# One-core transformer kernel: norm epsilon from a memset, first weight block in two transfers, and its copy moved between the two row tiles

## The reference, cut to what matters

```python
def _rmsnorm(x, g):
    x32 = x.astype(F32)
    y = x32 * lax.rsqrt(jnp.mean(x32 * x32, axis=-1, keepdims=True) + NORM_EPS)
    return (y * g.astype(F32)).astype(x.dtype)
...
def _moba(x, w_qkv, w_o):
    ...
    qkv = jnp.einsum('bsd,de->bse', x, w_qkv).reshape(b, s, 3, h, dh)
```

## Time and profile before

| | us |
|---|---|
| median of 3 runs | 826.84 (826.57 to 828.23) |
| profiled execution, its own time | 830.34 |
| its span in the trace | 828.6 |
| PE busy in the span | 769.8 |
| DVE busy | 486.1 |
| ACT busy | 375.4 |

### The profile page before, as it was taken

How to read it: one execution, slowest core, us unless ns; L and a number is a source line. 1 busy time by engine, 2 the same in 40 slices (tenths; PEclk the granted TensorE clock), 3 DMA queues, 4 the chain that set the end, 5 groups by cost and what they waited for, 6 DMA issues and landing times.

```text
span 828.6 us, 16218 instructions
## 1 busy us (share of the span) xinstructions
PE 769.8 (93%) x6678; PEld 646.5 (78%) x6678; DVE 486.1 (59%) x842; ACT 375.4 (45%) x572; POOL 55.0 (7%) x94
## 2 busy tenths in 40 slices
PE   7999999999999999999999999999999787686876
PEld 6999998999999998999998999899855443343432
DVE  4555667767766778857764344487875423324245
ACT  4555764554554556467553554464432212111123
POOL 2300041000000000200111000000010000000000
PEclk9999999999999999999999999999999988888789
DMA  9964362555555654534343132459989999999992
GB/s 301 293 206 138 117 191 77 202 179 175 202 168 187 203 170 136 198 108 153 121 136 100 56 103 102 153 163 403 420 330 421 420 421 419 421 420 420 420 418 84
DMA packets 89027, 193.82 MB, mean 234 GB/s; under 512 B 3630, under 2 KB 69521, under 8 KB 76546
## 3 DMA queue, kind: packets, MB, share of 16 engines
q1 hardware_dynamic: 86640, 186.66, 60.8%
q0 software_dynamic: 1888, 4.61, 1.8%
q10 hardware_dynamic: 434, 1.62, 0.5%
HBM read 191.83 MB, written 1.05 MB: 233 GB/s over the span
## 4 chain that ended last, share of the span: by engine, by line
PE 72%; DMA 18%; DVE 5%; ACT 2%; issue 1%; SPq 1%; DVEq 0%; ACTq 0%
DMA expert_w<-in_expert_w_up 17%; PE PG L2045 15%; PE PG L2047 14%; PE PG L2046 14%; PE PG L2654 3%; PE PM L2045 3%; PE PM L2047 3%; PE PM L2046 3%; PE PM L2684 2%; PE PM L2505 1%; ACT whi L853 1%; PE PG L2676 1%; SPq L679 1%; DMA raw<-in_moba_w_qkv 1%; PE PM L2130 1%
## 5 line engine op out<-in xcount | busy, mean ns | idle before, releaser
L2045 PE MATMUL PG<-hT_hi,whi 128*128 128x256 f32 (+1 forms) x816 | 235.5, 289 | 1.5 <-DVE hT_lo L1382 1.4
L2047 PE MATMUL PG<-hT_hi,wlo 128*128 128x256 f32 (+1 forms) x816 | 230.4, 282 | 0.0
L2046 PE MATMUL PG<-hT_lo,whi 128*128 128x256 f32 (+1 forms) x816 | 230.3, 282 | 0.0
L1364 DVE TENSOR_TENSOR wlo<-raw,whi 128x2048 fp32r<-128x2048 f32 x73 | 167.2, 2290 | 66.7 <-ACT whi L853 66.5
L2045 PEld LDWEIGHTS PG<-hT_hi,whi 128*128 128x128 f32 x816 | 153.8, 189 | 7.9 <-issue 4.6
L2047 PEld LDWEIGHTS PG<-hT_hi,wlo 128*128 128x128 f32 x816 | 154.1, 189 | 0.0
L2046 PEld LDWEIGHTS PG<-hT_lo,whi 128*128 128x128 f32 x816 | 153.6, 188 | 0.2
L853 ACT ACTIVATE whi<-raw 128x2048 fp32r<-128x2048 f32 x73 | 139.4, 1910 | 22.3 <-PE PG L2047 19.9
L2654 PE MATMUL PG<-expert_w,xw 128*32 128x256 f32 x992 | 75.4, 455 | 38.5 <-DMA expert_w<-in_expert_w_up 38.5
L2654 PEld LDWEIGHTS PG<-expert_w,xw 128*32 128x32 f32 x992 | 37.0, 126 | 61.6 <-issue 50.4
L1956 DVE SCALAR_TENSOR_TENSOR y_lo<-PG,small,y_hi 128x512 fp32r<-128x512 f32 x16 | 12.0, 750 | 97.5 <-ACT y_hi L1283 97.5
(11 more groups left out here) (529 smaller groups left out, 1339.2 us busy)
## 6 DMA issues: line engine op xcount, KB each, us to landing
expert_w<-in_expert_w_gate SPq DMA_DIRECT2D x32, 1024.0 KB, 26.6
expert_w<-in_expert_w_up SPq DMA_DIRECT2D x32, 1024.0 KB, 26.8
expert_w<-in_expert_w_down SPq DMA_DIRECT2D x32, 1024.0 KB, 26.8
raw<-in_ffn_w_up SPq DMA_DIRECT2D x22, 1024.0 KB, 5.0
raw<-in_w_in SPq DMA_DIRECT2D x22, 1024.0 KB, 5.0
raw<-in_moba_w_qkv SPq DMA_DIRECT2D x12, 1024.0 KB, 5.8
raw<-in_ffn_w_down SPq DMA_DIRECT2D x11, 1024.0 KB, 4.8
raw<-in_moba_w_o SPq DMA_DIRECT2D x4, 1024.0 KB, 5.1
```

The costliest lines, as they stand in the source:

```text
L1364: dve.tensor_tensor(lo_of(n), raw[:, n % R, :], hi_of(n).bitcast(F32), ALU.subtract).then_inc(s_lo, 1)
L2045: pe.matmul(dst, lh, rh, start=start, stop=False, **kw)
L2046: pe.matmul(dst, lh, rl, start=False, stop=False, **kw)
L2047: return pe.matmul(dst, ll, rh, start=False, stop=stop, **kw)
```

## The change

Three edits. The epsilon of the first norm is a column of `vrow` that POOL fills by a second memset, so ACT's square root waits for `s_row_mix` 18 (two memsets and the row `norm_mix`) in place of the constants. Granule 0 comes in two transfers of 128 x 4 x 256; the first half raises `s_first_hi`, the second `landed[0]`. ACT and DVE take the first half of granule 0 between the turned rows of tile 0 and those of tile 1. PE's order is the same.

```diff
-        ones_row = vrow[0:1, 0, :]
+        ones_row, eps_first = vrow[0:1, 0, :], vrow[:, 1, 0:1]
...
-            for i in range(12):
+            for i, done in enumerate((s_first_hi, landed[0])):
+                k = slice(KH * i, KH * i + KH)
+                sp.dma_start(raw[:, 0, GR // 2 * i:GR // 2 * i + GR // 2].rearrange("p (k n) -> p k n", k=KH), wqkv[:, k, 0:256]).then_inc(done, 16)
+            for i in range(1, 12):
...
             pool.memset(ones_row, 1.0).then_inc(s_row_mix, 1)
+            pool.memset(eps_first, RMS_EPS).then_inc(s_row_mix, 1)
...
-                    act.activation(rt[:, i:i + 1], ss[:, i:i + 1], ACT.Sqrt, scale=1.0 / D, bias=con("eps6")).then_inc(s_rt, 1)
+                    act.activation(rt[:, i:i + 1], ss[:, i:i + 1], ACT.Sqrt, scale=1.0 / D, bias=con("eps6") if q else eps_first).then_inc(s_rt, 1)
...
             norm_sq(0)
-            act.wait_ge(s_cst, 16)
+            act.wait_ge(s_row_mix, 18)
             norm_sqrt(0, [0])
             norm_sq(1)
             norm_sqrt(0, [1])
-            act.wait_ge(landed[0], 16)
+            norm_hi(0, [0])
+            act.wait_ge(s_first_hi, 16)
             act.activation(hi_of(0)[:, 0:GR // 2], raw[:, 0, 0:GR // 2], ACT.Copy).then_inc(s_first_hi, 1)
-            norm_hi(0)
+            norm_hi(0, [1])
+            act.wait_ge(s_cst, 16)
...
-                        dve.wait_ge(s_row_mix, 18)
+                        dve.wait_ge(s_row_mix, 19)
...
             norm_apply(0)
+            norm_lo(0, [0])
             c = slice(0, GR // 2)
-            dve.wait_ge(s_first_hi, 1)
+            dve.wait_ge(s_first_hi, 17)
             dve.tensor_tensor(lo_of(0)[:, c], raw[:, 0, c], hi_of(0)[:, c].bitcast(F32), ALU.subtract).then_inc(s_first_lo, 1)
-            norm_lo(0)
+            norm_lo(0, [1])
...
-            pe.wait_ge(s_row_mix, 17)
+            pe.wait_ge(s_row_mix, 18)
```

## The result

The change is **slower**: median 829.8 us (828.09 to 832.57, 11 runs) against 827.57 us (826.57 to 828.5, 11 runs of the kernel before beside it). The ratio is 1.0024, 95% interval 1.0014 to 1.0033, some 2 us. The forecast was no change, 827.2, with a range up to 828.6. The profiled execution took 832.57 us with a span of 830.8.

A forecast was written before the change was run, and what follows sets the result against it. PE was taken to bound the kernel (72% of the chain), its start held by granule 0's landing. Epsilon 0, transfers 0, order +0.36 and 0 behind it gave 827.2 us, called no change, range 825.8 to 828.6.

The forecast's parts named there:

- step 3 of the part on the order: On DVE: first half's lo waits for ACT's copy at 12.32, then runs 12.35 to 13.58.
- +0.36: New order on ACT and DVE: PE's first real multiplication starts at 14.32 against 13.96, 0.36 us later.
- The clock rival: PE's hole grows from 1.40 to 1.76, TensorE drops to 1.2 GHz: costs 2.15, 829.35 us; chance 0.07.
- The signs set beforehand: Changed profile: transposes at 8.78, first-half copy 11.3, PE 14.3; wrong if transposes move or copy starts before 11.
- The epsilon gains nothing: ACT's square root starts 1.09 earlier, but PE is in `keep_warm` until 8.78: gain on the path 0.
- Nothing between granule 0 and the experts absorbed the shift: No transfer stands on the chain there, so a shift of PE's start moves all that follows equally, once.
- The price of a second transfer: One more issue on SP ahead of granules 1 and 2: taken as 0, bounds 0 and 0.6 us.
- The late-landing rival: Granule 0 lands later in most runs, which only the kernel before pays fully: 825.8 to 827.2 us; chance 0.22.

The follow-up runs named there:

- Run 3: The change, with GpSimd's subtraction made to wait until DVE has done its own; ratio 1.0015 to the kernel before.
- before's second profile: The kernel before, unchanged, run and profiled again; PE starts at 13.51, first expert load at 558.24, ratio 0.9996.
- run 10: The kernel before, with PE also waiting for granule 1's lo and `keep_warm(24)` in place of `keep_warm(3)` filling the hole; ratio 1.0040.
- run 9: The kernel before, with PE also waiting for granule 1's lo before it starts granule 0, hole unfilled; ratio 1.0066 to the kernel before.
- the order alone: The kernel before with only the new order on ACT and DVE, epsilon and transfers as before; ratio 1.0019.
- run 4: The change with fourteen instead of three idle multiplications behind the transposes, filling PE's hole; ratio 1.0019 to the kernel before.
- run 7: The kernel before with only the epsilon taken from the memset; ratio 0.9997.
- run 8: The kernel before with only granule 0 split into two transfers; ratio 0.9997.

## Why the prediction was wrong

**What failed is step 3 of the part on the order**: "The lo of the first half waits for 12.32, runs 12.35 to 13.58". The wait was right, the 1.23 us was not. It came from a row of before in which DVE's subtraction began at 10.79 and POOL's at 10.86. DVE was first by 0.07, so its duration was undisturbed and POOL's 3.39 held a wait of 1.02 (3.39 less the 2.37 that it takes when it is first). In the new order POOL is first, and the wait falls to DVE, which is on the path. The rows that show the overlap were there to read, and POOL's 3.39 for a subtraction as large as DVE's of 1.23 was taken as its own speed. Run 3 shows it: POOL moved away, 1.23 is back.

**The size.** Counted from the constants, the forecast had PE's start at 7.41 (14.32 less 6.91). The change's profiles show 8.21, 7.95 and 8.23, later by 0.54 to 0.82, and DVE's subtraction is longer by 0.58 to 0.86: nothing else was mis-sized in the order. Against before's second profile (13.51) the start moved by 1.02 to 1.35, where +0.36 was forecast. At one to one (run 10) this is 0.12 to 0.16%. The measured interval, 0.14 to 0.33%, begins there. Of the 2.6 us between 827.2 and 829.8, 0.7 doesn't come from the change at all: the forecast stood on a median of three runs of the kernel before, 826.84, and eleven gave 827.57.

**The clock rival had 0.07 and came true in two of three profiles.** Its price was near: 2.15 forecast, 2.1 in run 9, and in the change's own profiles 2.9 (first load 4.13 behind before's second profile, 1.26 of it the start) and 1.6 (2.92 less 1.35). Its chance was set for a hole of 1.76; the conflict made it 1.9 to 2.6 in the change and 2.9 with the order alone. The Trainium skill, page "TensorE: Matmul & The Clock Gate", section "Part 1: The HAM clock gate", says that the windows over which the chip judges run freely and don't start with the kernel, so that the point of a change of level varies with where in a window the work falls. The runs agree in that like holes, 2.64 and 2.58, gave both outcomes.

How often does it fall in the runs behind the median? No trace shows them, but the record has each run's mean granted clock. In the change's two sets of 11 runs, the ten longest (829.80 to 832.57) have 0.967 or 0.968 and the twelve shortest (827.96 to 829.18) 0.969 to 0.971. The medians of these two groups are 830.46 and 828.34, 2.1 us apart, which is the price of run 9. With the hole filled, 1 run of 11 is under 0.969. This speaks for a fall in somewhat less than half of the change's runs, and for a loss made up of the later start and, in those runs, the clock. It is no proof: the mean takes in the whole span, before's first profile has 0.968 with the full level at 15 to 20, and 14 of 94 runs of the kernel before are under 0.969 too. And how much of the median is the clock's stays **open**, since run 4, whose runs hardly show a fall, is no faster than the change within 0.1%.

**The signs set beforehand.** Two of them came true by the letter: the transposes moved (8.43, not 8.78) and ACT's copy started before 11 (10.87). Neither was the fault. Counted from the constants the copy came at 4.31 where the forecast has 4.35 (11.26 less 6.91); the signs were set as absolute times, and the start of this profile was 0.35 earlier. The sign that did tell, multiplications at the spacing of the lower level, was the clock's. No sign was set on the length of DVE's subtraction.

**What held.** The epsilon gains nothing while `keep_warm` stands in front of the transposes (run 7). The transposes moved only with the constants: 8.43, 1.87 behind 6.56, as 8.78 behind 6.91. Nothing between granule 0 and the experts absorbed the shift. The price of a second transfer was taken as 0 and is no loss (run 8). The late-landing rival failed: landings do move by 0.44, but the granule and the constants moved together (2.79 apart in the first profile of before, 2.85 in the second), so neither order gains on the other in them.

## What to carry to other kernels

When an instruction is moved, look at what runs beside it at its new place, and don't take its duration from a row where it had started first: in these runs two subtractions with all operands in SBUF, one on DVE and one on GpSimd, ran one after the other. A duration that is long for its size, such as 3.39 us beside 1.23, may be a wait inside the busy time. And at the start of a kernel count from a common event, here the constants: they landed between 6.26 and 6.91 in the fourteen profiles, and the start of the change's PE, less what DVE's subtraction took over 1.23, was 7.37 behind them in all three profiles.

## What the runs showed of the hardware

DVE's subtraction with both inputs in SBUF and GpSimd's copy or subtraction, which read SBUF too, exclude each other for a whole instruction. The one that starts first runs at its own speed (DVE's 1.22 to 1.23, GpSimd's copy 1.04 and its subtraction 2.35 to 2.38). In seven profiles DVE's half-granule subtraction, started while GpSimd worked, ended 1.07 to 1.09 us after GpSimd's instruction (for example 12.95 and 14.02, 12.65 and 13.74, 10.14 and 11.21), and GpSimd's, started behind DVE's, ended 2.21 to 2.24 after it (before: 12.02 and 14.25). DVE's `hT_lo` pieces, with one operand in PSUM, kept their 0.68 to 0.69 beside GpSimd's work, though their other operand, `hT_hi`, is in SBUF. The wait shows inside the length of the blocked instruction and not as idle time in front of it. The Trainium skill, page "SBUF — State Buffer", section "SBUF: two separate sides", has this rule: a DVE operation with two SBUF inputs and a GpSimd operation that reads SBUF compete for an exclusive lock held for the whole instruction. The runs agree in every case. By that rule, with the durations of these runs on the forecast's own base, GpSimd's subtraction would end at 13.23 (10.86 + 2.37), DVE's at 14.3 and PE would start near 15.05 (0.75 behind DVE's end, as in the change), 1.1 later than before; the runs show 1.02 to 1.35.

TensorE's clock fell behind holes of 2.64 and 4.26 us, and about a microsecond after one of 1.90, but not behind holes of 2.58 and 2.88. When it rises at the start varies as well: the sixteen transposes took from 2.55 (run 4) to 3.62 us (third profile of the change). There the level is read from the spacing: in before the windows from 9.0 to 10.25 list a granted clock of 1.00 though the transposes start 0.21 apart.
